# A hybrid attention, pooling and mixture-of-experts block on one core: the query projection as 2x2 blocks with seven products, and other places for gate sums, scores, pooled means and turned probabilities

## The reference, cut to what matters

```
h = rms_norm(x, norm1_g)
proj = h @ w_in            # q 512 | k 128 | v 128 | qi 256 | ki 64 | wi 4 | pool 512 | gate_a 1024 | gate_p 1024
q = rope(rms_norm(q)); k = rope(rms_norm(k))
score = sum_h(relu(qi_h . ki) * wi_h) * IDX_SCALE      # the 64 best keys of each query are selected
attn = softmax(q . k * ATTN_SCALE over the selected keys) @ v
pooled = per-group linear map of (trailing mean - identity) * pool_scale
merged = sigmoid(gate_a) * (attn @ w_branch_attn) + sigmoid(gate_p) * (pooled @ w_branch_pool)
x = x + merged @ w_out
x = x + MoE(rms_norm(x))   # top 4 of 32 experts, each 1024 -> 2048 -> 1024
```

## Time and profile before

| | us |
|---|---|
| median of 3 runs | 1085.32 (1085.21 to 1085.86) |
| the profiled execution | 1084.87 |
| its span in the profile | 1082.8 |
| PE busy | 1047.1 |
| DVE busy | 390.4 |
| ACT busy | 123.5 |

### The profile page before, as it was taken

How to read it: one execution, slowest core, us unless ns; L and a number is a source line. 1 busy time by engine, 2 the same in 40 slices (tenths; PEclk the granted TensorE clock), 3 DMA queues, 4 the chain that set the end, 5 groups by cost and what they waited for, 6 DMA issues and landing times.

```text
span 1082.8 us, 12203 instructions
## 1 busy us (share of the span) xinstructions
PE 1047.1 (97%) x4826; PEld 423.7 (39%) x4826; DVE 390.4 (36%) x721; ACT 123.5 (11%) x218; POOL 15.2 (1%) x31
## 2 busy tenths in 40 slices
PE   8999999999999999999998989898989999899998
PEld 6445445434343434343433324242424333332432
DVE  3798885223232232232322222222222313132222
ACT  3115213100000000000000000000000100000001
POOL 4000000000000000000000000000000000000000
PEclk9999999999999999999999999999999999899999
DMA  9914897999999999999999999999999999999996
GB/s 328 372 40 155 328 412 264 410 430 418 427 429 427 428 429 434 432 432 425 429 435 429 428 429 431 431 431 434 433 430 430 431 432 431 427 432 425 428 430 276
DMA packets 37065, 430.44 MB, mean 398 GB/s; under 512 B 4225, under 2 KB 6401, under 8 KB 16433
## 3 DMA queue, kind: packets, MB, share of 16 engines
q1 hardware_dynamic: 35328, 427.59, 93.8%
q0 software_dynamic: 1136, 1.91, 0.5%
q10 hardware_dynamic: 576, 0.60, 0.2%
HBM read 429.03 MB, written 1.05 MB: 397 GB/s over the span
## 4 chain that ended last, share of the span: by engine, by line
PE 73%; DMA 24%; DVE 2%; issue 1%; SPq 1%; ACT 0%; ACTq 0%; DVEq 0%
PE bank L1677 31%; DMA ring<-w_gate_up_dram 21%; PE bank L1706 14%; PE bank L1602 5%; PE bank L1397 5%; PE bank L1258 4%; PE bank L1629 4%; DMA ring<-w_down_dram 3%; PE bank L1695 2%; PE bank L1556 2%; PE bank L1275 1%; PE bank L1222 1%; PE bank L1655 1%; PE bank L1281 0%; SPq L315 0%
## 5 line engine op out<-in xcount | busy, mean ns | idle before, releaser
L1677 PE MATMUL bank<-ring,scr 128*64 128x512 f32 x2032 | 476.1, 612 | 26.6 <-DMA ring<-w_gate_up_dram 26.4
L1677 PEld LDWEIGHTS bank<-ring,scr 128*64 128x64 f32 x2032 | 141.2, 140 | 324.4 <-issue 284.9
L1706 PE MATMUL bank<-ring,scr 128*64 128x512 f32 x992 | 225.0, 595 | 0.0
L1162 DVE TENSOR_TENSOR x<-bank,x 128x512 f32<-128x512 f32 x120 | 77.3, 686 | 254.8 <-PE bank L1629 254.8
L1706 PEld LDWEIGHTS bank<-ring,scr 128*64 128x64 f32 x992 | 68.9, 137 | 127.3 <-issue 122.9
L1137 DVE COPY scr<-bank 128x512 f32<-128x512 f32 x32 | 22.1, 692 | 256.9 <-PE bank L1677 256.9
L1143 DVE TENSOR_TENSOR scr<-bank,bgu 128x512 f32<-128x512 f32 x64 | 41.2, 686 | 98.5 <-PE bank L1695 98.5
L1629 PE MATMUL bank<-scr 64*128 64x512 f32 x240 | 67.7, 641 | 0.1
L593 ACT ACTIVATE scr<-bank 128x512 f32<-128x512 f32 x32 | 19.1, 597 | 383.1 <-PE bank L1677 383.1
L1602 PEld LDWEIGHTS bank<-scr,xn 128*128 128x128 f32 x480 | 54.8, 192 | 13.0 <-issue 13.0
L1602 PE MATMUL bank<-scr,xn 128*128 128x128 f32 x480 | 57.8, 278 | 0.0
(11 more groups left out here) (231 smaller groups left out, 533.0 us busy)
## 6 DMA issues: line engine op xcount, KB each, us to landing
ring<-w_gate_up_dram SPq DMA_DIRECT2D x40, 4096.0 KB, 31.4
ring<-w_down_dram SPq DMA_DIRECT2D x62, 2048.0 KB, 17.5
ring<-w_gate_up_dram SPq DMA_DIRECT2D x40, 2048.0 KB, 17.3
ring<-w_gate_up_dram SPq DMA_DIRECT2D x13, 1024.0 KB, 8.8
ring<-w_in_dram SPq DMA_DIRECT2D x12, 1024.0 KB
ring<-w_out_dram SPq DMA_DIRECT2D x4, 1024.0 KB
ring<-w_down_dram SPq DMA_DIRECT2D x4, 1024.0 KB, 29.0
ring<-w_branch_pool_dram SPq DMA_DIRECT2D x2, 1024.0 KB
```

The source lines that it names most:

```text
L1162: V.tensor_tensor(x[:, b, 512 * h:512 * h + 512], XY[h][:, :], x[:, b, 512 * h:512 * h + 512], ALU.add).then_inc(read[f"Y{j}"], 1)
L1677: ins = MM(GB[h][T * g:T * g + T, :], xgT[:, k, T * e:T * e + T], w[:, c0:c0 + 512], start=k == 0, stop=k == KC - 1)
L1706: ins = MM(DB[T * h:T * h + T, :], actT[e][:, c, :], v3(dn_slot[j][:, :], 4)[:, k, 512 * h:512 * h + 512], start=c == 0, stop=c == KC - 1)
```

## The change

The query projection (`projection(2)`) is replaced by `query_projection`: seven products of blocks, each with four matmuls of 256 columns, into banks 4, 5, 3 and 2. DVE makes four differences of weight blocks (`query_part`), three of them ahead of the key chain and the fourth within it. ACT copies four partial sums out (`query`), and DVE adds the rest from the banks (`query_add`, four instructions) ahead of the query chain. `part(0, 2)` moves from behind the query chain to ahead of the adds. The query chain's scratch moves from `ptb` to `half[4]`.

In the second gates, `scores(1, 0)` moves from slot 7 to slot 9, `scores(1, 1)` from 11 to 13, both `mix`, both `pooled` and the first two `turn_probs` two slots back; `turn_probs(1, 0, 0)` stands at 27, and the last three stand one product later in `pooling_branch`. There `attended(1)` stands behind the sixth product instead of ahead of it. On DVE, `gate_sum(0, 0, 1)` moves from behind the first selection to ahead of it. Counts of semaphores are shifted to fit.

```diff
@@ SP @@
-                    sp.wait_ge(job_ready, u + 1)
+                    sp.wait_ge(job_ready, u + 1 if u < 4 else u - 1)
@@ ACT @@
+            def query(product, i, b, signal, n):
+                act.wait_ge(block_prod, product)
+                nc.scalar.activation(query_out[i], bank[4][:, 0:256], ACT.Copy, scale=small[:, 128 + b:129 + b]).then_inc(signal, n)
+
+            query(1, 0, 0, block_copied, 1)
             root(132, 6, 2)
-            job(2, qq)
+            query(3, 2, 1, block_copied, 1)
+            query(5, 3, 1, block_copied, 1)
+            query(7, 1, 0, job_read, 2)
             root(140, 16, 3)
@@ DVE @@
+            def query_part(i):
...
+                if i == 0:
+                    dve.wait_ge(unit_in[4], 16)
+                else:
+                    dve.wait_ge(block_part, i)
+                if i == 1:
+                    dve.wait_ge(unit_in[5], 16)
+                elif i == 3:
+                    dve.wait_ge(block_prod, 1)
+                V.tensor_tensor(out, a, b, ALU.subtract).then_inc(block_part, 1)
+
+            def query_add(i, b, acc, product, copied, before):
+
+                dve.wait_ge(block_prod, product)
+                dve.wait_ge(block_copied, copied)
+                if before:
+                    dve.wait_ge(query_added, before)
+                V.scalar_tensor_tensor(out=query_out[i], in0=acc[:, 0:256], scalar=small[:, 128 + b:129 + b], in1=query_out[i],
+                                       op0=ALU.mult, op1=ALU.add).then_inc(query_added, 1)
+
+            for i in range(3):
+                query_part(i)
...
             root_and_reciprocal(132, 6, 1.0 / HD, 2)
+            query_part(3)
...
             part(0, 1)
+            part(0, 2)
+            query_add(0, 0, bank[5], 2, 1, 0)
+            query_add(3, 1, bank[3], 5, 3, 0)
+            query_add(2, 1, bank[3], 5, 2, 0)
+            query_add(2, 1, bank[2], 6, 2, 3)
+            dve.wait_ge(query_added, 4)
...
-            part(0, 2)
             part(1, 0)
...
+                if b == 0:
+                    gate_sum(0, 0, 1)
                 top = small[:, 196:204]
...
-                if b == 0:
-                    gate_sum(0, 0, 1)
@@ PE @@
-            for j in range(1, 4):
-                projection(j)
+            projection(1)
...
+                unit(4)
+                product(bank[4], a11, w11, True)
+                unit(5)
+                product(bank[5], a12, w21, True)
+                pe.wait_ge(block_copied, 1)
+                pe.wait_ge(sums_ready, 4)
+                pe.wait_ge(block_part, 3)
+                product(bank[4], s2, query_t2, False)
+                pe.wait_ge(job_read, 4)
+                product(bank[3], s3, t3, True)
...
+                product(bank[4], s1, query_t1, False)
...
+                product(bank[2], a22, t4, True)
...
+                product(bank[4], s4, w22, False)
+
+            query_projection()
+            projection(3)
...
-            gates(1, {4: [lambda: scores(0, 0)], 7: [lambda: scores(1, 0)], 11: [lambda: scores(1, 1)],
...
+            gates(1, {4: [lambda: scores(0, 0)], 9: [lambda: scores(1, 0)], 13: [lambda: scores(1, 1)],
```

More of the change, by code:

```diff
@@ L154, in block_kernel @@
         pool_a = [v3(pooledT_t, GROUPS)[:, 2 * k:2 * k + 2, b * P:b * P + P] for b in range(NB) for k in range(2)]
+        query_w = [v3(half[u], 4)[:, :, 256 * h:256 * h + 256] for u in (4, 5) for h in range(2)]
+        query_t1, query_t2 = v3(siga_t[:, 0:1024], 4), v3(siga_t[:, 1024:2048], 4)
+        query_out = [qq[:, b, 256 * h:256 * h + 256] for b in range(NB) for h in range(2)]
         att_p1, att_u2, att_u4 = hT_t[:, 0:512], hT_t[:, 1024:1536], hT_t[:, 1536:2048]
@@ L491, in job @@
                 for b in range(NB):
[L492 removed]
+                    act.wait_ge(job_ready, 2 * (j if j < 2 else j - 1) + b + 1)
                     n = groups[j][1]
@@ L690, in rope @@
                 x1, x2 = src[:, :, :, 0:half], src[:, :, :, half:2 * half]
-                t = [r[:, 0:NB * nh * half].rearrange("p (b h n) -> p b h n", b=NB, h=nh) for r in rtmp]
+                t = [tmp[:, 512 * j:512 * j + NB * nh * half].rearrange("p (b h n) -> p b h n", b=NB, h=nh) for j in range(4)]
                 V.tensor_tensor(t[0], x1, cb, ALU.mult)
@@ L1300, in _, with query_projection, product @@
             projection(0, lambda: turn_x(1))
-            for j in range(1, 4):
-                projection(j)
+            projection(1)
+            def query_projection():
+                w11, t3, w21, w22 = query_w
+                t4 = w11
+                def product(acc, lhs, rhs, fresh):
+                    for k in range(4):
+                        ins = MM(acc[:, 0:256], lhs[:, k, :], rhs[:, k, :], start=fresh and k == 0, stop=k == 3,
+                                 skip_group_check=not fresh)
+                    ins.then_inc(block_prod, 1)
+                unit(4)
[8 more added lines that the diff above has]
+                product(bank[3], s3, t3, True)
+                pe.wait_ge(block_copied, 2)
+                product(bank[4], s1, query_t1, False)
+                pe.wait_ge(block_part, 4)
+                product(bank[2], a22, t4, True)
+                pe.wait_ge(block_copied, 3)
+                product(bank[4], s4, w22, False)
+            query_projection()
+            projection(3)
             def turn_k():
```

76 lines of the change are left out of this document (41 added, 35 removed).

## The result

The changed kernel takes 1089.74 us (median of 7 runs, 1087.79 to 1090.61); the kernel before, in the same job, 1085.75 us (7 runs, 1085.21 to 1086.36). The ratio is 1.0032, with an interval from 1.0022 to 1.0042: 4.0 us slower. The forecast was 1089.0 us, range 1085.8 to 1090.4. The profiled execution is the quickest of the seven: 1087.79 us, span 1085.9, against 1084.87 and 1082.8 before.

A forecast was written before the change was run, and what follows sets the result against it. The prediction took PE's prelude, with DVE close behind, to set when the experts' weight stream starts and so the end. 1084.87 us plus 2.4 (late path) plus 1.7 (clock fall) gave 1089.0 us, range 1085.8 to 1090.4.

The forecast's parts named there:

- PE's query stage: Query projection on PE: 12.0 to 12.2 us instead of 13.7, PE 1.6 us earlier; weight differences cost at most 0.3 us.
- DVE ahead of the scores: Four adds before the first scores: 1.8 us plus 0.1 for part(0, 2); DVE there at 85.9 instead of 84.67 us.
- Slot 8: Second gates: PE arrives at 86.3 us, waits 3.0 us for gate_sum(0, 3), done at 89.3; pooled(1) ends at 107.5.
- The pooling branch: Third block product waits 0.8 us, starts at 120.0; attention sums start 2.4 us late at 133.06, and PE takes that over.
- The clock: After the slot 8 wait, granted clock falls once from 2.4 to 1.2 GHz, adding 1.7 us on PE before pooled(1).
- The sum: Whole execution: 1084.87 us profiled before, plus 2.4 us late path, plus 1.7 us clock, gives 1089.0 us.
- The wait without a fall: Rival: PE waits at slot 8 but the clock doesn't fall, giving 1087.3 us; chance 0.27.
- The other side: Rival: DVE reaches first scores in time, PE keeps 1.1 of the saved 1.6 us, giving 1083.8 us; chance 0.17.
- Two falls: Rival: the clock falls a second time at the third block product, 1.7 us more, giving 1090.7 us; chance 0.08.
- Bound: Expert loop ends with the weights' stream, which begins behind the prelude; prelude time on PE goes one to one into the end.

The follow-up runs named there:

- e5: Kernel before plus four dependent, unused 256-column adds on DVE ahead of the query chain, nothing else changed; 1087.48 us, ratio 1.0016.
- e12: e3 with turn_probs(1, 1, 1) back ahead of the third block product; 1087.41 us, ratio 1.0018.
- e3: Changed kernel with three matmuls of product 1 of the second gates done twice at slot 4, filling PE's wait; 1088.62 us, ratio 1.0030.
- e7: Changed kernel with its four query adds cut from 256 to 4 columns; 1088.54 us, ratio 1.0026.
- e8: Changed kernel run once more without any edit, in the job of the other experiments; 1089.06 us, ratio 1.0039.
- e1: Changed kernel with the second gates' list and pooling branch of the kernel before; new query stage, adds and moved gate sums stay; 1086.94 us, ratio 1.0012.
- e6: Changed kernel with only turn_probs(1, 1, 1) put back ahead of the third block product; 1090.44 us, ratio 1.0037.
- e10: Changed kernel with the maximum over the first scores taken three times instead of once, lengthening PE's wait at slot 8; 1093.42 us, ratio 1.0074.
- e2: Kernel before with only the new places and moved gate_sum(0, 0, 1), no query products or adds; 1086.85 us, ratio 1.0011.

## Why the prediction was right, point by point

- **PE's query stage.** 24.21 to 36.29 us, 12.1 us as forecast; the second half of the weights caused no wait, and the weight differences took nothing (`part(0, 1)` at 40.98 us).
- **DVE ahead of the scores.** Adds 1.88 us (forecast 1.8), first scores at 85.98 (85.9). The pair of gate sums took 1.49 us again, as in the earlier trace rows. Costing the moves of `part(0, 2)` and `gate_sum(0, 0, 1)` at nothing gave the right number but left their role untold. e5 shows that they had 0.43 and 0.17 us of cover; left behind the adds and the first selection, each would have stopped PE in the first gates.
- **Slot 8.** The wait is 2.93 us (3.0). `pooled(1)` ends near 107.6 us (107.5).
- **The pooling branch.** The third block product waits 0.47 us (0.8) and starts at 120.09 (120.0); the copy L942 comes at 122.52 (122.35), the attention sums at 133.06 (133.06). The distance grew by 2.63 us, in place of 2.4: at the second output product PE is 2.34 us late, and 2.54 at the first expert matmul. That the turn's place carries a part of it is shown by e12, 0.8 us. The path was right; the term was 0.2 us too small. That DVE's sum, not PE, sets it is shown by e3 and e7.
- **The clock, the step that was mis-sized.** I had it fall once in every execution, for 1.7 us. In the profiled one it didn't: 91.51 us has eight records in 3.70 us. The sum for that execution was 1.2 us too high (1089.0 against 1087.79). In traces of kernels with this wait, three of six show the fall, for 3.4 or 6.8 us (1.7 to 3.2 us of time). In the table, the six rows with a wait have an excess of 0.8 to 3.0 us over what their prelude explains, the seven without one -0.1 to 0.6. The profiled executions that show the wait and no fall (changed, e7, e8) lie only -0.6, 0.1 and 0.6 us above theirs. So the term is there in some executions, worth at most 1.4 us in the changed kernel's median and 0.8 in e8's. The mean granted clock, which each execution has, ties this to single executions. It is 0.984 or less in 24 of the 45 executions of kernels with the wait, in 2 of the 72 of kernels without one, and in 1 of 77 of the kernel before. In the changed kernel the five such executions have a median of 1090.01 us, the other two are at 1087.79 and 1088.53. In e1 the four at 0.984 are the four slowest of eleven, in e8 the two at 0.984 and 0.982 the slowest of five. So with this wait a lower clock comes in about half of the executions, and those are the longer ones; that it falls at slot 8 is seen only in the traces. It isn't all: the 21 executions with the wait at 0.985 or more still have a median excess of 0.7 us, against 0.1 without the wait. The expert loop, which was 0.9 us longer on average in the six traces with the wait (902.8 against 901.9 us), may hold that part; why it is longer isn't shown.
- **The sum.** 1089.0 us was counted from one execution of the kernel before (1084.87); from its median in the same job, 1085.75, it would be 1089.85, and 1089.74 was measured. That this is so close is in part luck: the path was 0.2 us more than forecast, the rest (1.4) 0.3 us less, and the rest is a mixture of executions with and without a fall, not one fall of 1.7 us in each.
- **The rivals.** The wait without a fall, 1087.3 us, describes the profiled execution (1087.79), not the median. The other side needed the gate sum by 86.3 us; e7, with 1.05 us less on DVE, still had a distance 1.59 us longer than before. Two falls didn't occur in a trace, but one of double length did (e6, and e10 behind its longer wait).
- **Bound.** Prelude time went into the end one to one: in the seven kernels without a wait, the medians follow the distances within 0.6 us.

Open is what decides whether this wait is followed by half clock, and why the expert loop took 901.5 to 903.5 us in the thirteen traces besides before's 901.6.

## What to carry to other kernels

Before a helper engine is given more to do, look for every place at which the bounding engine waits on it, not for the nearest: here the first gates had 0.43 and 0.17 us of cover, slot 8 had 1.1, and moving two instructions chose between them. That cover also hangs on which loads land first: in e2, whose DVE has no added work, PE waited at the first of these places too (`55.86 0.63 PE L1222 MATMUL bank<-consts,ring 128*128 128x128 f32 x4 [0.56 <-issue]`), as PE had started 0.49 us earlier and the load of `part(0, 0)` had landed 0.56 us later. When work is moved behind a wait, ask what it would have fed: the scores behind the gate sum cost more with the late sum than each edit alone. And the cure was cheap: issue the one sum that is waited for earlier, and put the waiting matmul's neighbours where their inputs are surely there.

## What the runs showed of the hardware

- The length of a wait alone didn't tell whether half clock followed. PE's waits at slots 7 and 8 of 2.05, 2.93 and 3.02 us had none, 1.82 us had 3.4 us of it, 2.82 us had 6.8 us, 5.22 us had 6.8 us. The earlier trace rows had suggested a limit between 1.99 and 2.37 us; e1 contradicts it. e8 and e6 stand in front of slot 8 alike, and differ. Nor did the fall come at a fixed time behind the start of the wait: by the stretches it began at 89.1 us in e1, 1.3 us after PE had resumed, at 89.3 in e6, 0.3 us before PE resumed, and at 89.2 in e10, 2.8 us before. The Trainium skill (TensorE: Matmul & The Clock Gate, "What's actually happening") calls the number of slow matmuls at the start of a kernel "run-variable", because what measures PE's activity runs free of the program. The traces here show the same for a wait in mid-kernel, which can end either way; that this is the reason no run here shows.
- Four adds from banks, of which only the last depends on the one before it, took 1.88 us at 256 columns and 0.83 us at 4: 0.21 us each is left when the work is almost gone. Four of 256 columns that each wait for the one before, with all inputs in the ring, took 2.04 us (e5).
- With identical code the prelude's distance came out at 145.38 us twice, where DVE was the bound, and at 141.94 and 141.33 us where PE was; whole executions of the changed kernel, in two jobs, differed by up to 4.5 us (1087.79 to 1092.27).
